# First norm's sums between the steps of the second projection, and the compressed keys' root behind GpSimd's third split

## The reference, cut to what matters

```python
def rmsnorm(x, g):
    y = xf * lax.rsqrt(jnp.mean(xf * xf, axis=-1, keepdims=True) + EPS)
    return (y * g.astype(jnp.float32)).astype(x.dtype)

def mixer_a(h, cos32, sin32, cos16, sin16, w_in, kv_norm, w_uk, w_uv):
    q, c_kv, k_rope, q_idx, k_idx, w_idx, q_mem = split_cols(h @ w_in, A_SPLITS)
    ...
    c_kv = rmsnorm(c_kv, kv_norm)
    ...
    w_idx = w_idx * (IDX_HEADS * IDX_DIM) ** -0.5
    o = dsa_attention(q_nope, q_rope, c_kv, k_rope, q_idx, k_idx, w_idx, w_uk, w_uv)

# in dsa_attention
        dots = jnp.einsum('bqhd,bsd->bqhs', qi, k_idx).astype(jnp.float32)
        score = jnp.einsum('bqhs,bqh->bqs', jax.nn.relu(dots), wi.astype(jnp.float32))
        ...
        _, idx = lax.top_k(score, topk)
```

## Time and profile before

| | |
|---|---|
| median of 3 runs | 2417.23 us (2413.25 to 2422.09) |
| profiled execution, its own time | 2415.6 us |
| its span in the profile | 2413.8 us |
| mean granted TensorE clock | 0.958 |
| PE busy | 2273.4 us (94%) |
| DVE busy | 1298.2 us (54%) |
| ACT busy | 921.1 us (38%) |
| POOL busy | 250.7 us (10%) |

### The profile page before, as it was taken

One profiled execution on the slowest core, in us unless ns is written; L12 is line 12 of the kernel. 1 busy time (PEld: TensorE's weight loads), 2 busy tenths in 40 slices (PEclk: granted clock), 3 DMA queues, 4 the chain that ended last, 5 costly groups with the idle time before them and its releaser, 6 DMA issues.

```text
span 2413.8 us, 34422 instructions
## 1 busy us (share of the span) xinstructions
PE 2273.4 (94%) x10882; PEld 1855.7 (77%) x10882; DVE 1298.2 (54%) x2537; ACT 921.1 (38%) x1850; POOL 250.7 (10%) x143
## 2 busy tenths in 40 slices
PE   7986999999999799999999999999999689999997
PEld 6675777888888687788888888888887667777766
DVE  5876444666644566466664454555544643545443
ACT  4433453322322266432223332222223334555551
POOL 0042221000001111110000210000002000011112
PEclk8998999999999999999999999999999889999888
DMA  3121111332333110223232332222222312000001
GB/s 131 51 88 53 61 53 62 96 101 90 104 102 102 66 36 26 77 90 99 93 104 96 104 97 96 99 99 96 96 96 79 113 63 85 2 19 9 19 10 70
DMA packets 50053, 182.93 MB, mean 76 GB/s; under 512 B 5552, under 2 KB 5680, under 8 KB 49840
## 3 DMA queue, kind: packets, MB, share of 16 engines
q1 hardware_dynamic: 49824, 181.35, 22.9%
q0 software_dynamic: 144, 0.52, 0.1%
HBM read 179.76 MB, written 2.10 MB: 75 GB/s over the span
## 4 chain that ended last, share of the span: by engine, by line
PE 83%; DVE 7%; issue 4%; ACT 3%; POOL 1%; DMA 1%; DVEq 0%; ACTq 0%; POOLq 0%; SPq 0%
PE pj L1863 68%; PE ps L2006 4%; PE po L2062 4%; PE pt L2022 2%; ACT w_hi L670 1%; DMA raw<-in_wstream 1%; PE po L2047 1%; PE ps L2176 1%; DVE s_sb L1303 1%; PE pj L1973 1%; DVE rtmp L1248 1%; DVE w_lo L1118 1%; PE po L2071 1%; ACT p_sb L757 1%; DVE rtmp L1245 1%
## 5 line engine op out<-in xcount | busy, mean ns | idle before, releaser
L1863 PE MATMUL pj<-h_hi,w_hi 128*128 128x512 f32 x1736 | 706.9, 407 | 21.0 <-DVE w_lo L1118 15.6
L670 ACT ACTIVATE w_hi<-raw 128x1024 fp32r<-128x1024 f32 x334 | 353.7, 1059 | 865.6 <-PE pj L1863 848.8
L1863 PE MATMUL pj<-h_lo,w_hi 128*128 128x512 f32 x1736 | 683.8, 394 | 0.0
L1863 PE MATMUL pj<-h_hi,w_lo 128*128 128x512 f32 x1736 | 683.6, 394 | 0.0
L1118 DVE TENSOR_TENSOR w_lo<-raw,w_hi 128x1024 fp32r<-128x1024 f32 x288 | 390.4, 1356 | 392.2 <-ACT w_hi L670 391.9
L1863 PEld LDWEIGHTS pj<-h_hi,w_hi 128*128 128x128 f32 x1736 | 331.1, 191 | 90.1 <-issue 17.1
L1863 PEld LDWEIGHTS pj<-h_hi,w_lo 128*128 128x128 f32 x1736 | 330.5, 190 | 71.1
L1863 PEld LDWEIGHTS pj<-h_lo,w_hi 128*128 128x128 f32 x1736 | 331.5, 191 | 64.6 <-issue 1.4
L1863 PE MATMUL pj<-G_hi,w_hi 128*128 128x512 f32 x704 | 278.1, 395 | 3.1 <-DVE G_lo L1367 3.0
L1863 PE MATMUL pj<-G_lo,w_hi 128*128 128x512 f32 x704 | 276.0, 392 | 0.0
L1863 PE MATMUL pj<-G_hi,w_lo 128*128 128x512 f32 x704 | 275.9, 392 | 0.0
(11 more groups left out here) (295 smaller groups left out, 2531.4 us busy)
## 6 DMA issues: line engine op xcount, KB each, us to landing
raw<-in_wstream SPq DMA_DIRECT2D x334, 512.0 KB, 3.4
xT<-in_x SPq DMA_DIRECT2D x4, 512.0 KB, 9.5
out_x<-xT SPq DMA_DIRECT2D x4, 512.0 KB, 2.7
memT<-in_mem SPq DMA_DIRECT2D x1, 1024.0 KB, 12.3
cst<-in_cst SPq DMA_DIRECT2D x1, 512.0 KB, 10.5
tab<-in_tab POOLq DMA_DIRECT2D x1, 512.0 KB, 5.0
posi<-in_pos SPq DMA_DIRECT2D x1, 256.0 KB, 2.8
vec<-in_vec SPq DMA_DIRECT2D x1, 182.5 KB, 2.4
```

The costliest lines, as they stand in the source:

```text
L670: nc.scalar.activation(w_hi[:, c.par * CW:(c.par + 1) * CW], raw[:, c.par * CW:(c.par + 1) * CW], ACT.Copy).then_inc(hi_ready, 1)
L1863: mm = nc.tensor.matmul(acc, w[:, col:col + P], x[part], start=first and k == 0, stop=last and k == 2)
```

## The change

On PE the 32 sums of the first norm now stand between the steps of `afront` 1, four behind each step. `spread("amix")` moves behind `idx_query(0, 0)`, and the `turn` of the index weights behind `idx_query(0, 1)`. On ACT the squares are cut in two groups of four around the split of chunk 2, and the squares of `mem`, the `widx` copy and one split trade places. On GpSimd the root of the compressed keys stands behind the third split. On DVE the same 16 rounds are cut 3, 5, 4, 4 where they were cut 6, 4, 2, 4. On PE `spread("ckv")` stands behind memory chunk 4.

```diff
@@ gpsimd
             for c in range(*POOL_CHUNKS["mem"]):
                 split_lo(At(c))
-                if c == CH["mem"] + 5:
+                if c == CH["mem"] + 2:
                     inverse_root("ckv")
@@ scalar
-            def squares(name, waits):
+            def squares(name, waits, start=0, stop=None):
                 src, n, _, _, _, _ = NORM[name]
-                for m in range(dict(NORMS)[name]):
+                for m in range(start, stop or dict(NORMS)[name]):
...
-            squares("amix", lambda m: (x_loaded[m // 2], 16))
             c, t = At(CH["afront"]), At(TL["afront"])
+            squares("amix", lambda m: (x_loaded[m // 2], 16), 0, 4)
             split_hi(c + 2)
             take(qn[:, 0:S], t, c)
+            squares("amix", lambda m: (x_loaded[m // 2], 16), 4)
             tables(0)
+            split_hi(c + 3)
             spread_factor("amix")
             act.wait_ge(ld["mem"], 16)
             for m in range(DT):
                 gained("mem", m // 2, m % 2)
-            split_hi(c + 3)
             split_hi(c + 4)
...
             idx_query(0, 0)
+            squares("mem", lambda m: (ld["mem"], 16))
             act.wait_ge(v_turned, TN["widx"] + 1)
             nc.scalar.activation(widx[:, :].rearrange("p (b c) -> p b c", b=NB), bank3(TN["widx"], 0, 16),
                                  ACT.Copy, scale=1024.0 ** -0.5)
-            squares("mem", lambda m: (ld["mem"], 16))
+            split_hi(At(CH["idx"] + 3))
             tables(1)
-            split_hi(At(CH["idx"] + 3))
             idx_query(0, 1)
@@ vector
-            rounds(6)
+            rounds(3)
             means("ckv")
             dve.wait_ge(rs_ready, STATS.index("ckv") + 1)
             nc.vector.tensor_tensor(rck[:, 0:NB], r4[:, 0:NB], rsa[:, 0:NB], ALU.mult).then_inc(rck_ready, 1)
+            rounds(5)
+            apply("ckv")
             rounds(4)
-            apply("ckv")
-            rounds(2)
             for part in range(2):
                 query(ATT["aq"], 0, 0, part)
             rounds(TOPK // 8 - 12)
@@ tensor
             project(At(CH["afront"]), At(TL["afront"]), h_hi, h_lo, norm="amix")
-            sums("amix")
-            pe.wait_ge(ld["cst"], 16)
-            for some in (range(4), range(4, CB)):
-                project(At(CH["afront"] + 1), At(TL["afront"] + 1), h_hi, h_lo, some=some)
-                if 0 in some:
-                    spread("amix")
+            for k in range(CB):
+                project(At(CH["afront"] + 1), At(TL["afront"] + 1), h_hi, h_lo, some=range(k, k + 1))
+                sums("amix", range(k, k + 1))
...
             idx_query(0, 0)
-            turn(At(TL["afront"] + 1), TN["widx"])
+            pe.wait_ge(ld["cst"], 16)
+            spread("amix")
             for k in range(CB):
                 idx_query(0, 1, range(k, k + 1))
                 sums("mem", range(k, k + 1))
+            turn(At(TL["afront"] + 1), TN["widx"])
...
-                if k == 5:
+                if k == 4:
                     spread("ckv")
```

## The result

| | before | after |
|---|---|---|
| median of the runs | 2416.69 us (2413.25 to 2422.09, 4 runs) | 2435.51 us (2433.55 to 2437.07, 4 runs) |
| span of the profiled execution | 2413.8 us | 2431.8 us |
| mean granted TensorE clock | 0.958 | 0.955 |

The changed kernel is slower, by under 1%: the ratio is 1.0075, with a 95% interval of 1.0055 to 1.0096. The forecast was 2433.6 us. The total is close to it, but it was not made up as the prediction said.

A forecast was written before the change was run, and what follows sets the result against it. The prediction took PE's pace to bound the kernel, with DVE holding up the first attention. Its terms, 2.4 + 6.4 + 7.4 + 0.2 = 16.4 us on the 2417.2 us median, gave 2433.6 us, range 2424 to 2441.

The forecast's parts named there:

- Sums between the steps: PE's head: eight steps of 1.6 us with four sums each, ending at 33.4; `idx_query(0, 0)` ends at 38.8.
- The clock in the mixed stretch: PE's mix of projection steps and sums: the clock falls there, +6.4 us, the middle of 3.3 and 9.6.
- The spread behind `idx_query(0, 0)`: Head: the spread loses its cover, so PE stands about 7.7 us and starts chunk 3 at 47.0.
- Chunk 3's projection: Head: 9.2 us plus 2.1 for an initial low clock and 0.4 for the turn; first index tile +2.4 us.
- The prediction's mark for the fall: Sign in the profile after: a granted clock of 0.50 in part of 24 to 45 us.
- The root behind the third split: Middle: root ready at 157.0 rather than 167.3, but DVE asks three rounds earlier; wait moves, by itself +0.8 us.
- `apply("ckv")` after eight rounds: Middle: DVE waits 7.4 us for `c_hi` in place of 0.9, then eight rounds follow instead of six; +7.4 us.
- The 0.2 us of the pipeline: Middle: the earlier root delays the fourth split by some 1.2 us; estimated 0.2 us at the first attention query's chunk's turn.
- The rest is free: Remaining edits: no cost from the earlier `spread("ckv")`, unchanged instruction counts on PE, DVE and POOL, no added DMA.
- the held clock: Rival on the head's mixed stretch: the clock does not fall, sum 10.0 us, time 2427.2 us; chance 0.27.
- The rival of `apply` not held: Rival on the middle: no wait holds `apply`, 2.4 to 8.8 us in all, 2419.6 to 2426.0 us; chance 0.08.
- that of a root wait that goes without another in its place: Rival on the middle: -8.9 us there, +2.4 in the head with the clock held, time 2410.7 us; chance 0.05.

The follow-up runs named there:

- e5_middle_late_apply: e2_middle_alone with two more rounds ahead of `apply`, so the rounds are cut 3, 7, 2, 4; 2415.52 us, ratio 0.9993 to the kernel before.
- e6_middle_rounds_first: e2_middle_alone with three rounds put between `means` and the root wait, six ahead of `apply`, none between it and the query; 2415.38 us, ratio 0.9981 to before.
- e3_head_warm: e1_head_alone plus 30 unused matmuls on PE between the spread of the first norm and chunk 3; 2418.13 us, ratio 1.0001 to the kernel before.
- e1_head_alone: The kernel before with only the change's head edits on PE and ACT, up to the index tiles; 2426.56 us, ratio 1.0029.
- e8_both_refitted: Middle of e6_middle_rounds_first; e1_head_alone's head with spread after step five of `idx_query(0, 0)`, chunk 3's low part and `mem` squares earlier; 2405.82 us, ratio 0.9946 to before.
- e2_middle_alone: The kernel before with only the early root, rounds cut 3, 5, 4, 4 and `spread("ckv")` behind memory chunk 4; 2424.34 us, ratio 1.0032.

## Why the prediction came out as it did

- *Sums between the steps.* Right: 1.6 us a step, the sums end at 33.2 for 33.4, `idx_query(0, 0)` at 38.8.
- *The clock in the mixed stretch.* **This step failed.** It put +6.4 us on a fall of the clock in the mix, as the middle of 3.3 and 9.6. Measured: 1.00 from 20.60 to 38.80, price 0. The neighbour that I chose, the bare sums at 0.50, did not carry over: with a projection step of 0.69 us between each four sums the clock held, as in the `mem` mix. On this stretch the Trainium skill's "TensorE: Matmul & The Clock Gate", section "HAM oscillation — how this bites in real kernels", which puts the fall down to idle gaps, was the better guide. It is not the whole story: the bare sums of before fell to 0.50 with PE busy 6.86 of 6.86 us.
- *The spread behind `idx_query(0, 0)`.* Right: a wait of 7.56 us for 7.7, chunk 3 at 46.98 for 47.0.
- *Chunk 3's projection.* **Mis-sized, and with the other error it is the heart of the head.** I let the low clock cost 2.1 us, after the 3.5 us at 0.52 of before. It cost 17.09 - 9.16 = 7.9 us: the clock did not return within the whole projection. With the turn at half clock this is nearly the 6.4 that I had put in the wrong place, so that 8.6 us stood against my 2.4 + 6.4 = 8.8 by a cancellation of two errors. So the first score, at 64.96 inside the range of 59 to 68, and the total are near by luck. The prediction's mark for the fall, a clock of 0.50 in part of 24 to 45 us, did not tell the two apart either: the clock was at 0.50 from about 42.2 us, but in PE's wait and not in the mix. Chunk 3's start does: with 6.4 us lost in the mix it would have been 53.4 and not 46.98.
- *The root behind the third split.* Right: 8.74 us of waiting in place of 8.90, after three rounds in place of six.
- *`apply("ckv")` after eight rounds.* Right: the two rounds cost 7.4 us (32.99 us from the end of the wait to `bias_a`, 25.61 before). Around it the bookkeeping was off by 1.4 us: `c_lo` came 8.1 us later than before and the first round 9.6. PE's work between the two ran faster than before; the `ckv` sums, whose rows follow, took about 1.8 us where before they took about 3.4. On DVE's side the root came earlier, but `rck` took 2.34 us (see the last section), and in sum `hf` ended 0.3 us later after the first round than forecast. So the wait for `c_hi` was 5.66 us for 7.4. PE's wait ahead of the first attention grew by the 7.4 us that were forecast, at the first scores (10.01 us for 2.64).
- *The 0.2 us of the pipeline* can't be told from this.
- *The rest is free*: nearly. About 1.0 us went between the first index score and the first round. In the profiled execution the clock was at 0.50 there until 66 us and from about 97 to 100 us, in that of before only from about 123 to 126 us; that this is the whole 1.0 us is not shown. The last 2.5 us lie far behind the change, in a stage at 1904 to 1937 us of before. From the first matmul of a projection (1904.40 before, 1919.58 after, 1901.54 in e5_middle_late_apply) to PE's restart behind DVE's `cmp_k` this stage takes 32.3, 34.8 and 34.9 us. Stretches that begin some 2.3 us ahead of that matmul, of before, after and e5_middle_late_apply in turn:

```profile
1902.00:1918.00 16.00, 14.54 (x70) 11.91 (x69) 11.01 (x20) 5.20 (x7) 0.00 (x0) 1.00 0.40 128
```

```profile
1917.30:1933.30 16.00, 13.72 (x55) 11.20 (x56) 9.63 (x17) 4.38 (x6) 0.00 (x0) 0.89 0.37 129
```

```profile
1899.30:1915.30 16.00, 13.76 (x55) 11.18 (x56) 9.62 (x16) 4.33 (x6) 0.00 (x0) 0.89 0.39 128
```

Before runs its stretch at 1.00, the other two at 0.89, since the first 3 us of the projection run at 0.50 there. e5_middle_late_apply, whose time is that of before, has this stage as the changed kernel has it. From `bias_a` to the end the profiled execution of before takes 2202.2 us, and those of the other nine kernels 2203.3 to 2207.7. So the profiled execution of before was short there; the change did not make it long.

PE's timeline of the `ckv` sums, before:

```profile
143.67 1.02 PE L1907 MATMUL ps<-ones,sq 128*128 128x1 f32 x4 [2.21 <-ACT sq L685]
144.55 0.99 PE L1907 MATMUL po<-ones,sq 128*128 128x1 f32 x4
```

And after:

```profile
153.24 0.61 PE L1908 MATMUL ps<-ones,sq 128*128 128x1 f32 x4 [2.21 <-ACT sq L685]
153.71 0.58 PE L1908 MATMUL po<-ones,sq 128*128 128x1 f32 x4
```

Of the rivals, the held clock is what happened in the mix, but not at its price: its 2427.2 us is 8.3 below the median, since it too took the 2.1. The rival of `apply` not held, and that of a root wait that goes without another in its place, did not happen here; e6_middle_rounds_first shows the second as a thing that can be had, by rounds ahead of the wait.

## What to carry to other kernels

An idle gap on TensorE costs its length and then, in what follows, perhaps more: here 7.6 us of waiting were bought back almost fully by a better order ahead of them, and the half clock behind them cost 7.9. Before a cover is taken from a wait, look at what runs after it, and count every input of that work, not the one that the profile names last. When a wait is moved forward in a list, count what then stands behind it, for the next wait there may end at a time of its own.

## What the runs showed of the hardware that I had not expected

- Chunk 3's projection with two sums per step (three matmuls of 512 columns and four of one) kept 1.00 when PE came to it busy (9.16 us in e3_head_warm), and stayed at 0.50 for 17.1 us when PE came to it from 7.56 us of idleness, with PE busy 17.09 of 17.09 us (the changed kernel and e1_head_alone). The level at the start does not settle it in every execution. With the head of before, PE came to this projection at 1.00 and had one wait of 0.97 or 0.98 us in it in all four profiled executions: in two the clock stayed at 1.00, in that of before it fell and was back after 3.5 us in the same mix, and in e6_middle_rounds_first it fell and stayed down for some 13 us.
- The same instructions at the same place met different clocks from one execution to the next: in four profiled executions with the head of before, the first index score started at 53.89, 55.16, 56.34 and 59.87 us. The kernel before ran from 2409.30 to 2425.08 us in 27 runs. Three kernels spread less: the changed one 3.5 us (4 runs), e3_head_warm 2.8 us (12) and e8_both_refitted 4.1 us (6). With 4 and 6 runs little can be said of a spread.
- `rck`, a DVE operation on 128x4, took 2.34 us where it took 0.16 and 0.38. It began at 164.92, 0.06 us after GpSimd's split at 164.86 (2.37 us), and ended with it, at 167.26 and 167.23. It was the same in e2_middle_alone and e5_middle_late_apply (2.33 us, begun 0.08 us after a split). In e6_middle_rounds_first and e8_both_refitted `rck` began when such a split had 0.4 and 0.3 us left, took 0.38 and 0.34 us, and again ended with it. By the Trainium skill's page "SBUF — State Buffer", section "Who interferes with whom", a DVE instruction with two SBUF inputs contends with a GpSimd instruction that reads SBUF. The rows agree: here the one begun first held the other until its end. So a tiny DVE operation with two inputs can cost as much as what is left of the GpSimd split beside it; in the changed kernel the wait for `c_hi` swallowed it.
